# The first gather of a mixture-of-experts stage split in two, a turn moved ahead of a product, and six weight pieces requested earlier

## What is computed

```
def hier_moe(h, w_rg, b_rg, w_re, b_re, w_g, w_u, w_d):
    t = h.reshape(-1, shp[-1])
    lg = t @ w_rg + b_rg                         # 4 groups, the best one is taken
    le = t @ w_re + b_re                         # 8 experts in it, the best two
    ...
    for g in range(N_GROUPS):
        a = jnp.einsum('td,edf->tef', t, w_g[g]) # 1024 -> 256 per expert
        u = jnp.einsum('td,edf->tef', t, w_u[g])
        out = out + jnp.einsum('tef,efd->td', jax.nn.silu(a) * u * comb[:, g, :, None], w_d[g])
```

## Time and profile before

| What | Value |
|---|---|
| median of 3 runs | 662.04 us (662.02 to 662.15) |
| the profiled execution | 661.96 us |
| its span, first to last instruction | 660.1 us |
| around the span | 1.9 us |
| granted PE clock, mean over the span | 0.997 of full speed |
| PE busy | 630.0 us, 95% |
| DVE, ACT, POOL busy | 53%, 39%, 19% |
| moved by DMA | 176.67 MB, mean 268 GB/s |

### The profile page before, as it was taken

How to read it: one execution, slowest core, us unless ns; L and a number is a source line. 1 busy time by engine, 2 the same in 40 slices (tenths; PEclk the granted TensorE clock), 3 DMA queues, 4 the chain that set the end, 5 groups by cost and what they waited for, 6 DMA issues and landing times.

```text
span 660.1 us, 9381 instructions
## 1 busy us (share of the span) xinstructions
PE 630.0 (95%) x3493; PEld 419.2 (64%) x3493; DVE 347.7 (53%) x739; ACT 255.0 (39%) x483; POOL 125.5 (19%) x139
## 2 busy tenths in 40 slices
PE   5999999998999999999999999999999999999985
PEld 3887888877888776778677878754433433343431
DVE  4649347995457565654456754665333424333312
ACT  5673343336424555565944324332221312221100
POOL 0018525663000310010000100021301401211211
PEclk9999999999999999999999999999999999999998
DMA  8975432364212833203967379999999999999991
GB/s 310 419 266 192 148 130 94 114 220 158 97 65 96 295 131 127 97 33 141 338 227 284 124 273 427 397 365 375 426 426 426 427 425 424 428 426 427 424 425 78
DMA packets 34720, 176.67 MB, mean 268 GB/s; under 512 B 4160, under 2 KB 4432, under 8 KB 21488
## 3 DMA queue, kind: packets, MB, share of 16 engines
q1 hardware_dynamic: 31696, 164.87, 63.3%
q0 software_dynamic: 2976, 11.16, 4.7%
HBM read 167.48 MB, written 9.06 MB: 267 GB/s over the span
## 4 chain that ended last, share of the span: by engine, by line
PE 77%; issue 9%; ACT 5%; DVE 4%; DMA 4%; POOL 0%; POOLq 0%; SPq 0%; ACTq 0%; DVEq 0%
PE banks L1986 15%; PE banks L1624 13%; PE banks L1626 13%; PE banks L1625 13%; PE banks L2009 8%; DMA piece<-in_wexp 4%; PE banks L1972 3%; ACT z L1075 1%; PE banks L1827 1%; ACT w_hi L955 1%; PE banks L1906 1%; DVE xs L1392 1%; DVE act_T L1420 1%; PE banks L1793 1%; PE banks L1800 1%
## 5 line engine op out<-in xcount | busy, mean ns | idle before, releaser
L1189 DVE TENSOR_TENSOR w_lo<-raw,w_hi 128x1024 fp32r<-128x1024 f32 (+1 forms) x81 | 128.3, 1596 | 74.2 <-ACT w_hi L955 74.0
L1624 PE MATMUL banks<-w_hi,hT_hi 128*128 128x512 f32 x312 | 124.8, 400 | 2.4 <-ACT z L982 1.8
L1626 PE MATMUL banks<-w_hi,hT_lo 128*128 128x512 f32 x312 | 122.0, 391 | 0.0
L1625 PE MATMUL banks<-w_lo,hT_hi 128*128 128x512 f32 x312 | 121.8, 390 | 0.0
L955 ACT ACTIVATE w_hi<-raw 128x1024 fp32r<-128x1024 f32 x79 | 83.5, 1057 | 90.9 <-PE banks L1626 87.2
L1986 PE MATMUL banks<-piece,xs 128*64 128x512 f32 x512 | 115.0, 593 | 2.5 <-DMA piece<-in_wexp 2.1
L1986 PEld LDWEIGHTS banks<-piece,xs 128*64 128x64 f32 x512 | 38.0, 137 | 75.6 <-issue 70.2
L1624 PEld LDWEIGHTS banks<-w_hi,hT_hi 128*128 128x128 f32 x312 | 58.7, 188 | 15.7 <-issue 2.9
L1626 PEld LDWEIGHTS banks<-w_hi,hT_lo 128*128 128x128 f32 x312 | 58.6, 188 | 12.6
L1625 PEld LDWEIGHTS banks<-w_lo,hT_hi 128*128 128x128 f32 x312 | 58.8, 188 | 11.1
L2009 PE MATMUL banks<-piece,act_T 128*64 128x512 f32 x256 | 58.5, 599 | 1.3
(11 more groups left out here) (345 smaller groups left out, 944.8 us busy)
## 6 DMA issues: line engine op xcount, KB each, us to landing
piece<-in_wexp SPq DMA_DIRECT2D x96, 1024.0 KB, 19.0
raw<-in_wstream SPq DMA_DIRECT2D x79, 512.0 KB, 3.5
foxc<-in_foxc POOLq DMA_DIRECT2D x8, 512.0 KB, 4.7
memv<-in_memc SPq DMA_DIRECT2D x8, 512.0 KB, 4.7
memk<-in_memc SPq DMA_DIRECT2D x8, 512.0 KB, 5.0
xT<-in_xT SPq DMA_DIRECT2D x1, 1536.0 KB, 11.2
xtok<-in_xtok SPq DMA_DIRECT2D x1, 1536.0 KB, 7.7
x<-in_xtok SPq DMA_DIRECT2D x1, 1536.0 KB, 7.3
```

What stands on the lines that cost most here:

```text
L1189: dve.tensor_tensor(w_lo[:, i % PART_SLOTS, cols], raw[:, i % RAW_SLOTS, cols], w_hi[:, i % PART_SLOTS, cols].bitcast(F32), ALU.subtract). ...
L1624: mm(out, xh, wh, start=start, stop=False, skip_group_check=True)
L1625: mm(out, xh, wl, start=False, stop=False, skip_group_check=True)
L1626: return mm(out, xl, wh, start=False, stop=stop, skip_group_check=True)
```

## The change

Four edits.

1. **Opening gather by pairs.** `pick` and the four `gather` steps of quad 0 become two times `pick_half` and two times two `gather_half`. Half a is the 128 places of pair a; its product has 128 columns, bank 5 holds channels 0 to 511 (copied out by ACT), bank 6 channels 512 to 1023 (DVE). Half 0 stands before `gu` of pair 0, half 1 behind it, ahead of `info 2` and `rows`. DVE writes the first half of `pick` ahead of the second `compact_low`.
2. **Slot weights.** `weights` is written ahead of `gu` of pair 0 instead of behind it.
3. **Turn ahead of the scatter.** In every pair that gathers, `hT_out` comes right after the gather products; the copies out of the gather (`gather_out`) come after it on ACT and DVE, and both halves of `scatter` after it on PE.
4. **Six pieces early.** `o_piece` gives pieces 0 to 5 places that are free sooner (and the gates other places in `z`), and SP requests piece 0 at `attention_done` and pieces 1 to 5 each behind one of the next `raw` granules. `x2` is requested behind them.

```diff
@@ moe_schedule @@
     plain("slots", 0)
+    plain("info", 1)
+    plain("pick_half", 0, 0)
     s.append(("compact_low", 0, 1, 1, None))
-    plain("info", 1)
-    plain("pick", 0)
-    for j, bank in enumerate((5, 6, 2, 3)):
-        step("gather", 0, j, bank)
+    for j in range(2):
+        step("gather_half", 0, j, 5 + j)
+    plain("pick_half", 0, 1)
+    plain("weights", 0)
     for p in range(PAIRS):
         ...
         step("gu", p, 0, 2 + p % 2)
         if p == 0:
-            plain("weights", 0)
+            for j in range(2):
+                step("gather_half", 1, j, 5 + j)
             plain("info", 2)
             step("rows", 0, 0, 7)
...
-        if pl < 2 or more:
+        gathers = pl < 2 or more
+        if gathers:
             q = 2 * g + 1 + pl // 2
+            outs = []
             for j in range(2 * (pl % 2), 2 * (pl % 2) + 2):
+                outs.append(("gather_out", q, j, ring[0], None))
                 ring_step("gather", q, j)
+            plain("hT_out", p)
+            s.extend(outs)
         if p:
             plain("scatter", p - 1, 0)
-        plain("hT_out", p)
+        if not gathers:
+            plain("hT_out", p)
         if p:
             plain("scatter", p - 1, 1)
@@ program, places @@
-        o_piece = [o_z + 8 * KB * i for i in range(12)] + ...
+        o_piece = [o_z + 8 * KB * i for i in (9, 10, 11, 4, 5, 3, 0, 1, 2, 6, 7, 8)] + ...
-        Z_OF = {C_RQK: 0, C_RV: 1, C_RG: 2, C_FQ: 3, C_FK: 4, C_FV: 5, C_MQ: 6}
-        GATE_SLOT = [3, 4, 6, 0, 1, 2]
+        Z_OF = {C_FQ: 0, C_FK: 1, C_RV: 2, C_RG: 3, C_RQK: 4, C_FV: 5, C_MQ: 6}
+        GATE_SLOT = [0, 1, 6, 4, 2, 3]
@@ SP @@
                 if kind == "k" and i + RAW_SLOTS < NGRAN:
                     granule(i + RAW_SLOTS)
+                    early = i - FIRST[C_BR + 3] + 1
+                    if early == 5:
+                        sp.wait_ge(br_add, 6)
+                    if 1 <= early < 6:
+                        load_piece(early)
+                    elif early == 6:
+                        load(x2[:, :, :], io["xtok"], s_x2)
...
                 elif kind == "attention_done":
                     sp.wait_ge(u_v, NU)
-                    load(x2[:, :, :], io["xtok"], s_x2)
+                    sp.wait_ge(br_add, 3)
+                    load_piece(0)
                 elif kind == "residual" and i == 0:
                     sp.wait_ge(mt_ready, 8)
-                    for c in range(12):
+                    for c in range(6, 12):
                         load_piece(c)
@@ PE, gather_half and down @@
+                elif what == "gather_half":
+                    pe.wait_ge(pick_ready, a + 1)
+                    pe.wait_ge(xg_lo_ready, j + 1)
+                    for k2 in range(4):
+                        k = 4 * j + k2
+                        for x in (xg_hi, xg_lo):
+                            ins = mm(ps[:, b0, P * k2:P * k2 + P], x[:, k * P:(k + 1) * P], pick[:, P * a:P * a + P], start=x is xg_hi, stop=x is xg_lo, **kw)
+                    ins.then_inc(gather_done, 1)
...
                     if a:
                         pe.wait_ge(ylo_ready, 2 * a)
+                    else:
+                        pe.wait_ge(*xs_of(1, 3))
+                        pe.wait_ge(*xs_of(1, 7))
```

More of the change, by code:

```diff
@@ L459, in program @@
         pT = at("pT", [P, 2, 256], o_work + 21 * KB)
-        o_piece = [o_z + 8 * KB * i for i in range(12)] + [o_raw + (16 + 8 * i) * KB for i in range(3)] + [o_h + (8 + 8 * i) * KB for i in range(2)]
+        o_piece = [o_z + 8 * KB * i for i in (9, 10, 11, 4, 5, 3, 0, 1, 2, 6, 7, 8)] + [o_raw + (16 + 8 * i) * KB for i in range(3)] + [o_h + (8 + 8 * i) * KB for i in range(2)]
         piece = [at(f"piece{i}", [P, 2048], o_piece[i]) for i in range(PIECES)]
@@ L637, in program @@
         NGROUP = group_of(NU - 1) + 1
-        rqk, rv, rg, fq, fk, fv, mq = (z[:, i, :, :] for i in range(7))
+        rqk, rv, rg, fq, fk, fv, mq = (z[:, Z_OF[c], :, :] for c in (C_RQK, C_RV, C_RG, C_FQ, C_FK, C_FV, C_MQ))
         POSTED = {C_MK: 1, C_RQK: 2, C_RG: 3, C_FQ: 4, C_FK: 5, C_MQ: 6}
@@ L791, in overflow_weights, with xs_of @@
             chain(dve.tensor_tensor(over, r_member[:, :, 0, 0:32], r_member[:, :, 1, 0:32], ALU.add))
+        def xs_of(p, k):
+            if p < 2:
+                return (xs_odd if k // 4 else xs_even), 2 * p + k // 2 % 2 + 1
+            return (xs_odd if k // 2 % 2 else xs_even), 2 * (p // 2) + 2 + k // 4 + 1
         def rows_of(g):
@@ L1133, in _ @@
                     ins.then_inc(xs_even, 1)
+                elif what == "gather_half" and j == 0:
+                    act.wait_ge(gather_done, 2 * a + j + 1)
+                    for k in range(4):
+                        ins = act.activation(xs[:, 0, k, P * a:P * a + P], ps[:, bank, P * k:P * k + P], ACT.Copy, scale=gk[:, 16 + k:17 + k])
+                        if k % 2:
+                            ins.then_inc(xs_even, 1)
                 elif what == "silu":
@@ L1378, in _ @@
                         dve.scalar_tensor_tensor(xg_lo[:, cols], xrow[a % 2][:, cols], r_mine[:, 5:6], xg_hi[:, cols].bitcast(F32), ALU.mult, ALU.subtract).then_inc(xg_lo_ready, 1)
+                elif what == "pick_half":
+                    dve.wait_ge(info_out, 2)
+                    cols = slice(P * j, P * j + P)
+                    chain(dve.tensor_scalar(pick[:, cols], cst2("iota1")[:, cols], r_mine[:, 0:1], None, ALU.is_equal))
+                    dve.scalar_tensor_tensor(pick[:, cols], cst2("iota1")[:, cols], r_mine[:, 1:2], pick[:, cols].bitcast(F32), ALU.is_equal, ALU.add).then_inc(pick_ready, 1)
+                elif what == "gather_half" and j == 1:
+                    dve.wait_ge(gather_done, 2 * a + j + 1)
+                    for k in range(4, KT):
+                        ins = dve.tensor_scalar(xs[:, 0, k, P * a:P * a + P], ps[:, bank, P * (k - 4):P * (k - 4) + P], gk[:, 16 + k:17 + k], None, ALU.mult)
+                        if k % 2:
+                            ins.then_inc(xs_odd, 1)
                 elif what == "pick":
                     dve.wait_ge(gather_done, 4 * a)
-                    dve.wait_ge(info_out, a // 2 + 3 if a else 2)
+                    dve.wait_ge(info_out, a // 2 + 3)
                     ids = cst2("iota1")[:, 256 * (a % 2):256 * (a % 2) + 256]
@@ L1385, in _ @@
                     dve.scalar_tensor_tensor(pick[:, :], ids, r_mine[:, 1:2], pick[:, :].bitcast(F32), ALU.is_equal, ALU.add).then_inc(pick_ready, 1)
-                elif what == "gather" and j % 2 == 1:
+                elif what == "gather_out" and j % 2 == 1:
                     dve.wait_ge(gather_done, 4 * a + j + 1)
@@ L1928, in bank_free @@
                 if what == "gather":
-                    pe.wait_ge(xs_odd if j % 2 else xs_even, 2 * a + j // 2 + 1)
+                    pe.wait_ge(*xs_of(2 * a, 2 * j))
+                elif what == "gather_half":
+                    pe.wait_ge(*xs_of(a, 4 * j + 3))
                 elif what == "compact":
@@ L1965, in _ @@
                     ins.then_inc(rows_ready, 1)
+                elif what == "gather_half":
+                    pe.wait_ge(pick_ready, a + 1)
[5 more added lines that the diff above has]
+                    ins.then_inc(gather_done, 1)
                 elif what == "gather":
-                    pe.wait_ge(pick_ready, a + 1)
+                    pe.wait_ge(pick_ready, a + 2)
                     pe.wait_ge(xg_lo_ready, 2 * (a // 2) + j // 2 + 1)
@@ L1978, in _ @@
                         if k % 2 == 0:
-                            pe.wait_ge(xs_odd if k // 2 % 2 else xs_even, 2 * (a // 2) + k // 4 + 1)
+                            pe.wait_ge(*xs_of(a, k))
                         for e2 in range(2):
```

## The result

| | before | after |
|---|---|---|
| median of 6 runs of each, us | 662.38 (662.02 to 664.27) | 666.05 (663.21 to 667.07) |
| ratio | | 1.0043, 95% interval 1.0025 to 1.0061 |
| the profiled execution, us | 661.96 | 666.82 |
| its span, us | 660.1 | 665.0 |
| granted PE clock, mean | 0.997 | 0.990 |

A forecast was written before the change was run, and what follows sets the result against it. Transfers at 425 GB/s were taken as the bound, their stream started by `down` of pair 0. Gather +1.8 us, turn -0.55 and early pieces 0 put it 1.2 later: 662.04 + 1.2 = 663.2 us, range 660.8 to 665.2.

The forecast's parts named there:

- Bound and order of work: From about 460 us transfers at 425 GB/s bind; every us the stream's start moves also moves the end.
- Six pieces early, 0: Opening: six pieces requested early fit the slow stretch but spare no later piece its slot wait; worth 0, cost 0.
- 128-column products, 0.11 us: Opening gather on PE: each float32 product of 128 columns takes 0.11 us, from row L1850.
- A: Rival, second half of the gather: 128-column products at 0.17 us or a longer DVE chain, 664.0 to 665.2; chance 0.30.
- B: Rival, split gather: 0.056 us a product, added half costs 0.9 less, 662.2 us; chance 0.12.
- The second half of the gather, +1.8 us: Between `gu` and `gu_rest` of pair 0: 16 added products and four DVE copies start `gu_rest` 1.8 us later.
- the 1.0 that was forecast: Opening: with the gather by pairs, `gu` of pair 0 starts 1.0 us earlier, at 436.0.
- PE idles about 1.6 us behind `info 2`: Opening, ahead of `rows`: PE's wait for DVE grows to about 1.6 us from 0.70.
- rival D: Last pairs: PE waits longer, its clock falls and two runs of 3.65 us in the tail double, 670.5 us; chance 0.02.
- The turn, 0.55 us back: Pair 0, ahead of the scatter: DVE's copy starts sooner behind the turn, shortening PE's 1.09 us wait by 0.55.
- for 19 ... 636.3. The largest wins: Slot releases: piece 21's bound, 638.0, exceeds piece 19's 636.3, so `down` of pair 0 starts the stream, 1.7 us to spare.
- The sum: `down` of pair 0 and the whole stream behind it 1.2 us later (1.8 - 0.55): 663.2 us.

The follow-up runs named there:

- e1: Kernel before with the six early pieces alone: 662.41 us, ratio 0.9997.
- e2: Kernel before with the opening gather by pairs and the early slot weights alone: 665.58 us, ratio 1.0049.
- e13: Whole changed kernel plus three unread products ahead of the 36-column products: 664.94 us, ratio 1.0049.
- e12: Kernel before with only three unread 384-column products ahead of the 36-column products: 661.58 us.
- e4: Changed kernel with six unread 512-column products filling PE's pause behind `info 2`: 663.26 us, ratio 1.0012.
- e9: e8 with four unread 512-column products directly ahead of `down` of pair 0: 662.15 us.
- e10: e8 with four unread 512-column products directly ahead of `gu_rest` of pair 0: 662.12 us.
- e3: Kernel before with the turn ahead of the scatter alone: 662.05 us, ratio 0.9996.
- e5: Kernel before with three extra 128-column DVE copies ahead of the reduction that `rows` waits for, lengthening PE's pause: 663.20 us, ratio 1.0020.
- e6: Changed kernel with `info 2` moved ahead of the second half of the opening gather: 662.24 us, ratio 1.0002.
- e7: Kernel before with the turn ahead of the scatter and opening gather banks in the order 5, 2, 6, 3: 662.16 us, ratio 0.9996.
- e8: e7 plus three unread 384-column products in PE's 0.47 us wait ahead of the 36-column products: 661.32 us, ratio 0.9983.
- e15: e6 plus three unread products ahead of the 36-column products: 661.47 us, ratio 0.9988.
- e17: Second series of e8 with a quarter of pair 0's `gu_rest` moved ahead of `rows`: 660.64 us, ratio 0.9964.
- e14: e5 plus three unread products ahead of the 36-column products: 662.54 us, ratio 1.0012.

## Why the prediction was wrong

**Bound and order of work: right.** The bytes set the end, the stream from 460 us kept its 426 GB/s, and every us of the opening came out at the end: G 4.97 later, the last `gu_rest` 4.95.

**Six pieces early, 0: right** (e1). `x2` and the `raw` granules weren't late.

**128-column products, 0.11 us: right** (0.11 in 32 of them); rivals A and B, which lived on another price, fall. B counted its saving of 0.9 us in the second half alone and gave no reason for leaving out the first. The Trainium skill (TensorE: Matmul & The Clock Gate, Back-to-back issue gap) gives the 56 ns cited beside the forecast for an isolated product, and about 81 ns for a stream of 128-column products with their loads. The trace agrees with neither: 110 ns.

**The second half of the gather, +1.8 us: over-sized, and a term was missing.** In e2 and in e13 `rows` starts at 442.99 and 442.98 against 441.82: +1.2, or +1.5 against e12's 441.49. DVE's four copies took 1.04 us (442.08 to 443.12) and not 1.3, which is the difference to 1.5; the pause was 1.45, not 1.6. The other 0.3 lie ahead of the change: `gu` started at 435.67 in both, 0.3 earlier than worked out, but 1.04 ahead of e12's 436.71, the 1.0 that was forecast. The profiled execution of before began its gather 0.3 us later than e12's.

**The step that failed** stands in the same paragraph: "PE idles about 1.6 us behind `info 2`, where it idled 0.70". I priced the pause as idle time alone. It was followed by `rows` and `gu_rest` at 1.2 GHz, which cost 0.5 and 2.55 us more in the profiled execution; e4 takes the fall away and lands on 663.26, 2.8 us lower. e13 has the fall in the pause and no other: 664.94, 1.7 us above that. The profiled execution of the changed kernel has two things more, the other fall at 422 us and a longer low stretch from the pause on (6.8 us against e13's 3.4); they are the likely source of the rest. I had looked for a fall of the clock in rival D, at the far end, where PE waits 1.19 us for a piece between long runs of 512-column products, and gave it 0.02. In the profile that I had, the nearest row for the pause was the 0.70 us behind `info 2`; it says that 0.70 is harmless and nothing about twice that. The 1.09 us ahead of `info 3`, harmless too, stands behind 256-column products, and the 1.19 us in the tail was harmless as well; none is as long as 1.45. The bound on this term should have been open upward, `gu_rest` at double length, 3.6 us.

**The turn, 0.55 us back: the local effect right (0.48 in every trace), its worth wrong.** The step is "for 19 ... 636.3. The largest wins", with 1.7 us to spare. I had counted only pieces for each release. From 446.09, when SP requests pieces 19 and 20, to 452.68, when it requests 21, are 6.6 us, and the two pieces fill 4.9 of them; the 1.7 us left are what I took for slack, but rows fetched and latency fill them: between G and 15 us behind it the DMA share is 0.97 at 372 GB/s, in the kernel before:

```profile
446.09 0.80 SPq L814 DMA_DIRECT2D piece<-in_wexp  x2
...
445.98:460.98 15.00, 13.91 (x74) 6.40 (x73) 8.45 (x27) 3.46 (x8) 2.93 (x4) 1.00 0.97 372
```

By an estimate from these figures, the same bytes at 425 GB/s would take 13.1 us, 1.9 less. The two releases are level. e9, e10 and the column L less G show it.

**The sum was right by luck, out of two errors.** +1.8 and -0.55 made +1.2; measured is +1.2 to +1.5 and -0.1, and e4 is 1.1 above before. The 663.2 of e4 doesn't confirm the terms.

**The rest of the difference** in the profiled execution, 0.8 us ahead of `rows`, is the fall at 423 us. The traces show it in five other kernels without the three products (e1, e3, e5, e6, e7) and in none of those with them. It most likely explains before's runs at 664 us too, and it isn't the change's.

## What to carry to other kernels

When an edit lengthens a wait of an engine whose granted clock can fall, price what runs behind the wait at both of its levels, and fill the wait with the kernel's own work (here a quarter of the next products, or the small product moved ahead of the added ones) before anything else. When several releases feed one full-rate stream, the latest by request time plus bytes isn't the only one that counts: as long as they are within what other transfers take between them, an earlier one pays only if all come earlier. And a few unread products that keep the clock steady turned a spread of 3 us into one of 0.6 to 1.7 (e8, e9, e10, e12, e15, e17), which is what makes small terms measurable.

## What the runs showed of the hardware that I had not expected

- PE's clock fell to half in a pause of 1.45 us and stayed there through about 5 us of uninterrupted 512-column products before it rose again (low from 443.2 to 450.0 us in the changed kernel); the fall costs more than the pause. Behind e5's pause of 1.48 us it fell only 1.3 us after the products had started again.
- Each fall in these traces is low for 3.4 us (e13's in the pause and e5's behind it; at 422 us the changed kernel, e3, e6, e7) or for 6.8 us (the changed kernel's in the pause; e1 and e5 at 422 us). The one of 3.4 us in e13 cost 1.7 us.
- Whether it falls varies from execution to execution of the same program, and no run shows why. By time and mean clock these are 38 of 145 at 422 us in the kernel before, short ones not counted, 4 of 12 behind the pause of e14, and 6 of 6 behind that of e13.
- A fill of three 384-column products in a pause of 0.47 us ended the long falls at 422 us: none of the 68 executions of e8, e9, e10, e12, e15 and e17 is above 663.2 us. Whether it ended every short one is open: one execution of e12 (662.67 us at 0.995) and one of e17 (661.94 at 0.994) stand 1.1 and 1.3 us above their medians at a lower mean clock.
